# A two-layer hybrid trunk: the rope branch's queries and keys transposed on VectorE instead of TensorE

## The reference

```python
h = rms_norm(x, g_pre_mix)
(a_u, a_v, b_q, b_k, b_v, c_b, c_c, c_x,
 d_cq, d_ckv, d_kr, gate_logits) = split_columns(h @ w_in)
out_a = chunked_sgu(gelu(a_u), gelu(a_v), a_ln_g, a_ln_b, a_w_s, a_b_s)
out_b = moba_attention(partial_rope(b_q), partial_rope(b_k), b_v)   # 4 heads of 64, causal
out_c = short_conv_mixer(c_b, c_c, c_x, c_w_conv)
out_d = mla_attention(d_cq, d_ckv, d_kr, d_q_norm_g, d_w_uq, d_kv_norm_g, d_w_ukv, ...)
merged = sum_i sigmoid(gates[i]) * (branches[i] @ w_branch[i])
x = x + rms_norm(merged @ w_out, g_post_mix)
y = square(relu(rms_norm(x, g_pre_mlp) @ w_mlp_in)) @ w_mlp_out
x = x + rms_norm(y, g_post_mlp)
```

## Time and profile before

| | |
|---|---|
| median of 3 runs | 791.15 us (790.91 to 791.2) |
| span of the profiled execution | 788.9 us; its own whole time is not listed, the median of the runs is 2.2 us above its span |
| PE busy | 781.6 us of the span (99%) |
| DVE busy | 506.3 us (64%) |
| ACT busy | 407.6 us (52%) |
| granted TensorE clock | 0.999 of full speed over the span |

### The profile page before, as it was taken

One profiled execution on the slowest core, in us unless ns is written; L12 is line 12 of the kernel. 1 busy time (PEld: TensorE's weight loads), 2 busy tenths in 40 slices (PEclk: granted clock), 3 DMA queues, 4 the chain that ended last, 5 costly groups with the idle time before them and its releaser, 6 DMA issues.

```text
span 788.9 us, 11019 instructions
## 1 busy us (share of the span) xinstructions
PE 781.6 (99%) x4053; PEld 659.3 (84%) x4053; DVE 506.3 (64%) x706; ACT 407.6 (52%) x631; POOL 62.3 (8%) x86
## 2 busy tenths in 40 slices
PE   9999999999999999999999999999999999999997
PEld 6898778888888888888889987878888888888885
DVE  5677655559777556555666876554788856565663
ACT  7566656443575445443546575554436745444441
POOL 1210000006110000000020100000333000000000
PEclk9999999999999999999999999999999999999999
DMA  9696555554466656567826855555654675656531
GB/s 310 187 304 190 160 161 157 176 202 133 149 198 216 209 178 190 191 188 220 275 66 199 281 162 160 158 163 187 186 157 140 200 225 185 187 185 207 179 119 53
DMA packets 88200, 145.86 MB, mean 185 GB/s; under 512 B 10316, under 2 KB 51556, under 8 KB 88164
## 3 DMA queue, kind: packets, MB, share of 16 engines
q1 hardware_dynamic: 88020, 145.24, 59.3%
q10 hardware_dynamic: 144, 0.13, 0.1%
HBM read 144.31 MB, written 1.05 MB: 184 GB/s over the span
## 4 chain that ended last, share of the span: by engine, by line
PE 99%; DVE 0%; POOL 0%; ACT 0%; POOLq 0%; issue 0%; DVEq 0%
PE banks L1352 24%; PE banks L1354 24%; PE banks L1353 24%; PE banks L1400 11%; PE banks L1401 5%; PE banks L1404 2%; PE banks L1585 1%; PE banks L1448 1%; PE banks L1466 1%; PE banks L1403 1%; PE banks L1364 1%; PE banks L1440 1%; PE banks L1410 1%; PE banks L1372 0%; PE banks L1438 0%; PE banks L1518 0%
## 5 line engine op out<-in xcount | busy, mean ns | idle before, releaser
L860 DVE TENSOR_TENSOR w_lo<-raw,w_hi 128x1024 fp32r<-128x1024 f32 (+1 forms) x256 | 306.3, 1225 | 123.8 <-ACT w_hi L529 123.4
L529 ACT CAST w_hi<-raw 128x1024 fp32r<-128x1024 f32 (+1 forms) x256 | 257.0, 1041 | 107.5 <-PE banks L1404 46.3
L1352 PE MATMUL banks<-w_hi,xT_both 128*128 128x512 f32 (+2 forms) x472 | 183.1, 388 | 0.0
L1354 PE MATMUL banks<-w_hi,xT_both 128*128 128x512 f32 (+2 forms) x472 | 178.6, 378 | 0.0
L1353 PE MATMUL banks<-w_lo,xT_both 128*128 128x512 f32 (+2 forms) x472 | 178.4, 378 | 0.0
L1400 PE MATMUL banks<-xT_both,w_hi 128*128 128x512 f32 x364 | 130.4, 398 | 0.0
L1352 PE MATMUL banks<-w_hi,brT_hi 128*128 128x512 f32 x320 | 125.4, 392 | 0.0
L1354 PE MATMUL banks<-w_hi,brT_lo 128*128 128x512 f32 x320 | 124.7, 390 | 0.0
L1353 PE MATMUL banks<-w_lo,brT_hi 128*128 128x512 f32 x320 | 124.7, 390 | 0.0
L1352 PEld LDWEIGHTS banks<-w_hi,xT_both 128*128 128x128 f32 x472 | 88.8, 188 | 18.6 <-issue 1.7
L1354 PEld LDWEIGHTS banks<-w_hi,xT_both 128*128 128x128 f32 x472 | 88.7, 188 | 16.4
(11 more groups left out here) (202 smaller groups left out, 757.0 us busy)
## 6 DMA issues: line engine op xcount, KB each, us to landing
raw<-in_w_in_dram SPq DMA_DIRECT2D x88, 512.0 KB, 4.6
raw<-in_w_mlp_in_dram SPq DMA_DIRECT2D x64, 512.0 KB, 4.7
raw<-in_w_mlp_out_dram SPq DMA_DIRECT2D x64, 512.0 KB, 4.3
raw<-in_w_branch_dram SPq DMA_DIRECT2D x16, 512.0 KB, 4.3
raw<-in_w_out_dram SPq DMA_DIRECT2D x16, 512.0 KB, 3.5
gate_th<-in_w_in_dram SPq DMA_DIRECT2D x8, 512.0 KB, 8.5
raw<-in_w_in_dram SPq DMA_DIRECT2D x8, 352.0 KB, 6.5
x<-in_x_dram SPq DMA_DIRECT2D x4, 256.0 KB, 4.2
```

The source lines that it names most:

```text
L529: nc.scalar.copy(w_hi[:, c % RING, h * n:(h + 1) * n], raw_of(q)[:, 0:n]).then_inc(hi_ready, 1)
L860: v.tensor_tensor(w_lo[:, c % RING, cut], raw_of(q)[:, 0:n], w_hi[:, c % RING, cut].bitcast(F32), ALU.subtract).then_inc(lo_ready, 1)
L1352: nc.tensor.matmul(dst, l_hi, r_hi, start=first, stop=False)
L1354: return nc.tensor.matmul(dst, l_lo, r_hi, start=False, stop=last)
```

## The change

The eight PE transposes of a layer and ACT's two copies are taken out. In their place DVE does sixteen transposes in each layer, each of one 32-token quadrant by one 32-feature quadrant, for both halves of tokens and all four groups of 128 features at once (queries two, keys two). They stand in four groups of four behind the subtractions of chunks 10, 11, 12 and 13. `qTB` and `kTB` become the two halves of one tensor `qkTB`. PE waits for DVE's last transpose (`qkTB_ready`) where it waited for ACT's copies, and behind chunk 10 for `wsT_copied` alone, which it now needs first there.

```diff
@@ sb
-        qTB = sb("qTB", [P, FT, S])
-        kTB = sb("kTB", [P, FT, S])
+        qkTB = sb("qkTB", [P, 2, FT, S])
+        qTB, kTB = qkTB[:, 0], qkTB[:, 1]
@@ ACT, side_step, s == 6
-                    for n, dst in enumerate((qTB, kTB)):
-                        act.wait_ge(qkTB_psum, nth(l, 2, n))
-                        nc.scalar.copy(dst.rearrange("p f n -> p (f n)"), psum[:, 6 + n, :]).then_inc(qkTB_copied, 1)
@@ DVE
+        BLOCKS = [(a, b) for a in range(4) for b in range(4)]
+            def qk_transpose(l, blocks):
+
+                if blocks[0] == BLOCKS[0]:
+                    dve.wait_ge(ropeB_ready, nth(l, 1, 0))
+                    if l > 0:
+                        dve.wait_ge(attn_psum, nth(l - 1, 4, 1))
+                for a, b in blocks:
+                    rows_a, rows_b = slice(32 * a, 32 * a + 32), slice(32 * b, 32 * b + 32)
+                    last = v.transpose(
+                        qkTB[rows_b].rearrange("p n f (t c) -> p t (n f) c", t=T)[:, :, :, rows_a],
+                        proj[rows_a, :, MIX:3 * MIX].rearrange("p t (g c) -> p t g c", c=P)[:, :, :, rows_b])
+                if blocks[-1] == BLOCKS[-1]:
+                    last.then_inc(qkTB_ready, 1)
@@ DVE, loop over s
                         side_step(l, s)
                         split(l, s + 3)
+                    if 7 <= s < 11:
+                        qk_transpose(l, BLOCKS[4 * (s - 7):4 * (s - 6)])
@@ PE, pair_scores, p == 0
-                    pe.wait_ge(qkTB_copied, nth(l, 2, 1))
+                    pe.wait_ge(qkTB_ready, nth(l, 1, 0))
@@ PE, side_after
-                if c == 5:
-                    pe.wait_ge(ropeB_ready, nth(l, 1, 0))
-                    pe.wait_ge(wsT_copied, nth(l, 1, 0))
-                    for n in range(2):
-                        for f in range(FT):
-                            for t in range(T):
-                                o = MIX * (1 + n) + f * P
-                                last = nc.tensor.transpose(psum[:, 6 + n, f * S + t * P:f * S + (t + 1) * P],
-                                                           proj[:, t, o:o + P], ident)
-                        last.then_inc(qkTB_psum, 1)
@@ PE, side_after, c == 10
-                    pe.wait_ge(qkTB_copied, nth(l, 2, 1))
+                    pe.wait_ge(wsT_copied, nth(l, 1, 0))
```

More of the change, by code:

```diff
@@ L213, in hybrid_trunk @@
         ropeB_ready = sem("ropeB_ready")
-        qkTB_psum = sem("qkTB_psum")
-        qkTB_copied = sem("qkTB_copied")
+        qkTB_ready = sem("qkTB_ready")
         av_squared = sem("av_squared")
```

## The result

The changed kernel takes **793.65 us** (median of 5 runs, 793.19 to 794.66), against 791.15 us (790.77 to 791.29, 5 runs) for the kernel before on the same chip: a ratio of 1.0034, with a 95% interval of 1.0023 to 1.0046. The profiled execution took 793.65 us itself, over a span of 791.9 us at a granted clock of 0.998. Its span is 3.0 us longer than that of before. The kernel before was profiled in a rather short execution: in later runs its spans of 789.1 and 789.5 us went with times of 790.88 and 791.29 us, so 788.9 us belongs to about 790.7 us (an estimate from these two).

What follows compares the result with a forecast made beforehand. PE's queue was taken to bound the kernel: -1.92 us freed, +1.74 and +1.54 waiting for the rotation, +0.34 for the tanh, so +1.70; span 790.6, time 792.8 us. The range ran from the full gain (789.2) to 797 us.

Steps and rivals of the forecast that it cites:

- The 2.2 us that I added around the span: Whole kernel: time taken as 2.2 us above the profiled span, turning 790.6 us into 792.8 us.
- What PE is offered: PE's queue: removing eight transposes a layer frees 1.05 us in layer 0 and 0.87 in layer 1, together 1.92 us.
- The price of a transpose: DVE: each of sixteen transposes a layer costs p, 0.45 us long and starting about 0.48 us apart.
- the memset rows: Profile rows of memsets, taken as agreeing that a quadrant change holds an instruction until earlier ones finish.
- two passes: Rival on DVE: a 4-byte element takes two passes, p = 0.75, giving 801.5 us; chance 0.17.
- the first rival: On DVE transposes overlap, p about 0.34 to 0.37, nobody waits, 1.92 us gained, 789.2 us; chance 0.15.
- The estimate of p = 0.477: DVE: a transpose's price from the skill page's 311 ns against 285 ns, fill about 26 ns; same result within 0.1 us.
- The path to the rotation: DVE, chunk 10 to branch D's rotation: ready at 67.55 + 16p in layer 0; PE waits 1.74 and 1.54 us.
- The second gate tanh: ACT, chunk 14: the tanh, queued behind the delayed work, makes PE wait some 0.17 us more per layer.
- The latents' wait for POOL: DVE: ACT's earlier squares remove a 0.91 us wait before scaling the latents in layer 1; no such wait in layer 0.
- the forecast's own formula: PE's wait for branch D's rotation: 16p - 5.94 us in layer 0 and 16p - 6.14 us in layer 1.

Runs made afterwards that it cites:

- e2: Changed kernel with DVE's sixteen transposes also removed (scores computed from zeros, a tiny memset raises the semaphore): 789.35 us, ratio 0.998.
- e3: Changed kernel with PE's eight transposes per layer put back, their result unread: 793.17 us, ratio 1.0038.
- e8: Changed kernel with each group of four transposes reading and writing the same 32 partitions, blocks wrongly placed: 790.52 us, ratio 0.9994.
- e5: Changed kernel with ACT's second gate tanh moved ahead of the first head's exponentials: 793.08 us, ratio 1.0024.
- e1: Changed kernel run again without any edit: 793.97 us, ratio 1.0038.
- e6: Changed kernel, two transpose groups behind chunks 11 and 13, two in step 12 behind rotation and `u_inner`, gate tanh ahead of exponentials: 789.24 us, ratio 0.9977.
- e10: Changed kernel with transpose groups behind chunks 11 and 13 and two in step 12, ACT's tanh not moved: 792.9 us, ratio 1.0026.

## Why the prediction was right

The mechanism was the forecast one, and the time of 793.65 us lies 0.85 us above the forecast of 792.8. In spans the forecast was further off: +1.7 us against +3.0. The 2.2 us that I added around the span were too many, since span and time of one execution lie 1.8 us apart (789.1 and 790.88, 791.9 and 793.65); that hid 0.45 us of it.

- **What PE is offered.** Forecast 1.05 and 0.87 us, measured 1.05 and 0.88. e2 shows that nearly all of it can be had, and e3 that it is worth nothing while DVE is late.
- **The price of a transpose.** Forecast 0.48 us (a length of 0.45, a gap of 0.03), measured 0.445 (a length of 0.436, a gap of 0.01). The choice among the rivals was right: there is no overlap when the quadrant changes, as the memset rows said, and there are not two passes. The size was 7% too high. e8 shows the overlapping case of the first rival on the same instructions: 0.34 us, just that rival's figure. The time was then 790.5 us and not that rival's 789.2: at 0.34 us the rival had nobody waiting, but in e8's profile the latents waited in both layers, and PE for the rotation and for the tanh. The estimate of p = 0.477 beside the forecast is 0.474 by its own figures (418 + 26 + 30 ns); no term rests on it.
- **The path to the rotation.** From the end of chunk 10's second half, 16.17 + 16p was forecast (67.55 - 51.38, and the transposes), 23.3 us at the measured price. It took 23.56 and 23.39 us. That DVE would fill its idle time and then work solidly was right but for 0.17 us in layer 0. There chunk 13's second half came late, which the forecast had excluded ("ACT has them rounded at about 60 and 61.4"): ACT waited for its load and had it rounded at 64.34.

```profile
63.28 1.06 ACT L529 CAST w_hi<-raw 128x1024 fp32r<-128x1024 f32 x1 [1.73 <-DMA raw<-in_w_in_dram]
```

- **The second gate tanh.** Forecast 0.17 us a layer, measured 0.40 and 0.39. This term was mis-sized: 0.11 us of it is PE's restart, which I had not counted, and the rest is 0.1 us out of lengths that I had added up over 10 us. e5 takes the wait out.
- **The latents' wait for POOL.** This step of mine failed: "These come 0.94 us earlier, so I let DVE's stretch in layer 1 begin 0.91 us earlier. In layer 0 DVE does not wait there." The wait does not hang on ACT's squares alone, but on whether POOL's addition behind them starts before DVE's L1037 or after it (e1), and it came in layer 0 instead. It makes the latents, and all of DVE's work behind them, 1.00 us later in layer 0 (2.13 instead of 1.13 us behind the subtraction's start). PE shows 0.29 us of it in chunk 10, where I had said that it does not wait earlier.
- **The start.** PE's work is 0.57 us later by 37 us in the profiled execution. By 12 us the shift is 0.53 us, and in the other profiles of changed kernels it was between 0.08 and 1.21 us there, so it varies from execution to execution. e2, where nothing else is left, is 0.1 to 0.3 us above the full gain; that bounds what of it could be lasting.

The sum at the measured price (0.447 us, the mean distance of the starts): -1.92 offered, +1.21 and +1.01 us of waits by the forecast's own formula (16 x 0.447 less 5.94 and 6.14), and +0.79 for the two tanhs make +1.09. The latents add 1.00, the longer path in layer 0 (23.56 instead of 16.17 + 7.15 = 23.32) 0.24, PE's restart behind the two rotations 0.06 each, and the start 0.57. That is 3.02, against 2.98 in the traces. Of the span's 3.0 us the medians show 2.5: the profile of before stretches the difference by about half a microsecond, as its execution was a short one.

So errors largely cancelled, and that the forecast came as close as 0.85 us is in part luck. The price was too high by 0.033 us, worth 1.1 us, and the tanh and the latents were too low by 1.5 us; the path, the restarts and the start, 0.9 us together, were not in the sum at all, and the 2.2 us around the span gave half of that back. That the 0.91 us is no property of the program could have been suspected from the earlier trace rows, since only one of two equal layers shows it.

What stays open: whether DVE's instruction really holds POOL's, as the order of their starts suggests, and why the load of chunk 13 was late in layer 0. A version of the original placement where the latents never wait was not run.

## What to carry to other kernels

Work that moves from the bounding engine to one with idle time is free only up to the slack at the next hand-over on each path that it is put ahead of; here 16 x 0.445 us = 7.1 us met a slack of 5.9 to 6.1, and the whole gain of 1.9 us and more was lost. Put such work directly behind the hand-over that is tight, and then look at what is queued behind it on every other engine: here one tanh on ACT had to stand ahead of an instruction that waited for the delayed one. Both moves together gave 4.4 to 4.7 us for the same instructions (e6 against the changed kernel); the placement alone gave 0.8 to 1.1 (e10), the tanh alone 0.6 to 0.9 (e5). A wait that is hidden now and shows in only one of two equal layers must be counted as possible in both, since it costs its full length as soon as the slack is gone (1.00 us on DVE's path in layer 0 here).

## What the runs showed of the hardware

- A float32 transpose of 32 x 256 on VectorE takes 436 ns (median) when it writes another group of 32 partitions than the instruction before it, and 394 ns when it stays on the same one (e8); they start 0.445 and 0.34 us apart. I had expected the gap to differ, not the length.
- The length of 436 ns is only 18 ns above an instruction of 256 elements without a transpose (418 ns), and the 394 ns of e8 are below it: the 0.03 us for filling a block that the forecast added do not show as a time of their own.
- GpSimd's power over 128 x 4 elements takes 1.87 us mostly and 1.34 to 1.46 us at times (18 and 6 of 24), and changes between the layers of one execution. In all 24 cases it ends 0.87 to 0.88 us behind the end of the VectorE instruction that was running when it started, one with two inputs in SBUF each time.
